# Rope's rotation in a three-layer block: a permutation product on TensorE, or four transfers inside SBUF

## The reference

```python
def apply_rope(x, cos, sin):
    half = HEAD_DIM // 2                     # HEAD_DIM is 64
    x1, x2 = x[..., :half], x[..., half:]
    c, s = cos[None, :, None, :], sin[None, :, None, :]
    out = jnp.concatenate([x1 * c - x2 * s, x2 * c + x1 * s], axis=-1)
    return out.astype(x.dtype)

for i in range(DEPTH_2):                     # 2
    hn = rmsnorm_2(h, norm_g[i])
    if i % N_MIXERS == 0:
        q, k, v, z = split_proj(hn, w_in_a[j], N_KV_A)      # 16 heads of queries, 2 of keys
        q, k = apply_rope(q, cos, sin), apply_rope(k, cos, sin)
        o = sliding_window_sink_attention(q, k, v, sinks_a[j])
    else:
        q, k, v, z = split_proj(hn, w_in_b[j], N_KV_B)      # 16 heads of queries, 4 of keys
        q, k = apply_rope(q, cos, sin), apply_rope(k, cos, sin)
        o = moba_attention(q, k, v)          # causal attention at this length
    h = h + (o * silu(z)) @ w_out[i]
return rmsnorm_2(h, final_g)
```

## Time and profile before

| | |
|---|---|
| Time, 3 runs | 797.45 us median (796.12 to 802.04) |
| Profiled execution | 795.86 us, span 793.9 us |
| TensorE busy | 733.2 us (92% of the span) |
| VectorE busy | 542.9 us (68%) |
| ScalarE busy | 366.6 us (46%) |
| GpSimd busy | 128.7 us (16%) |
| Window layer | about 557 to 672 us of the span |
| Causal layer | about 672 to 782 us |

### The profile page before, as it was taken

One profiled execution on the slowest core, in us unless ns is written; L12 is line 12 of the kernel. 1 busy time (PEld: TensorE's weight loads), 2 busy tenths in 40 slices (PEclk: granted clock), 3 DMA queues, 4 the chain that ended last, 5 costly groups with the idle time before them and its releaser, 6 DMA issues.

```text
span 793.9 us, 14919 instructions
## 1 busy us (share of the span) xinstructions
PE 733.2 (92%) x6112; PEld 685.8 (86%) x6112; DVE 542.9 (68%) x783; ACT 366.6 (46%) x564; POOL 128.7 (16%) x81
## 2 busy tenths in 40 slices
PE   5699999999977999887999999999999988999984
PEld 4489999999976898777999999999888778988884
DVE  3588979777785437667559548456789966788841
ACT  4253334433443436625434343436666665565532
POOL 0053111332222724221005000001300000000000
PEclk9799999999986999988999999999999999999998
DMA  9997799876658767335657664745443334343301
GB/s 308 349 304 239 237 350 301 267 248 213 224 185 288 248 226 248 108 124 172 209 184 265 212 192 133 253 163 158 137 130 107 107 106 159 112 155 109 104 2 53
DMA packets 132455, 152.64 MB, mean 192 GB/s; under 512 B 2616, under 2 KB 126268, under 8 KB 132284
## 3 DMA queue, kind: packets, MB, share of 16 engines
q1 hardware_dynamic: 132324, 152.01, 58.9%
q10 hardware_dynamic: 88, 0.02, 0.0%
HBM read 150.97 MB, written 1.05 MB: 191 GB/s over the span
## 4 chain that ended last, share of the span: by engine, by line
PE 68%; DVE 15%; ACT 10%; issue 4%; DMA 2%; POOL 0%; SPq 0%; DVEq 0%; ACTq 0%; POOLq 0%
PE sc L1353 10%; PE sc L1355 10%; PE sc L1354 10%; PE acc L1353 9%; PE acc L1355 8%; PE acc L1354 8%; DVE wlo L911 5%; ACT whi L601 3%; PE stat L1364 2%; DVE prob L1088 2%; DMA ada<-in_w_ada_dram 2%; ACT probT L734 1%; PE tp L1404 1%; ACT prob L727 1%; DVE prob L1108 1%
## 5 line engine op out<-in xcount | busy, mean ns | idle before, releaser
L911 DVE TENSOR_TENSOR wlo<-raw,whi 128x2048 fp32r<-128x2048 f32 x105 | 258.2, 2463 | 113.1 <-ACT whi L601 112.9
L601 ACT ACTIVATE whi<-raw 128x2048 fp32r<-128x2048 f32 x105 | 200.2, 1908 | 74.6 <-PE sc L1355 61.2
L1353 PE MATMUL sc<-nhi,whi 128*128 128x256 f32 x704 | 200.0, 284 | 6.0 <-DVE nlo L944 4.1
L1354 PE MATMUL sc<-nlo,whi 128*128 128x256 f32 x704 | 198.6, 282 | 0.0
L1355 PE MATMUL sc<-nhi,wlo 128*128 128x256 f32 x704 | 198.6, 282 | 0.0
L1353 PEld LDWEIGHTS sc<-nhi,whi 128*128 128x128 f32 x704 | 134.0, 190 | 7.4 <-issue 4.5
L1354 PEld LDWEIGHTS sc<-nlo,whi 128*128 128x128 f32 x704 | 135.6, 193 | 0.0
L1355 PEld LDWEIGHTS sc<-nhi,wlo 128*128 128x128 f32 x704 | 134.6, 191 | 0.0
L1353 PE MATMUL acc<-nhi,whi 128*128 128x256 f32 x376 | 110.8, 295 | 5.6 <-DVE nlo L944 2.7
L519 POOL TENSOR_TENSOR ada<-ada,cpad 128x2048 f32<-128x2048 f32 x16 | 73.3, 4583 | 244.0 <-DMA ada<-in_w_ada_dram 244.0
L1354 PE MATMUL acc<-nlo,whi 128*128 128x256 f32 x376 | 105.6, 281 | 0.0
(11 more groups left out here) (209 smaller groups left out, 1151.8 us busy)
## 6 DMA issues: line engine op xcount, KB each, us to landing
ada<-in_w_ada_dram SPq DMA_DIRECT2D x28, 1024.0 KB, 5.2
raw<-in_w_gate_dram SPq DMA_DIRECT2D x22, 1024.0 KB, 5.9
raw<-in_w_up_dram SPq DMA_DIRECT2D x22, 1024.0 KB, 5.5
raw<-in_w_down_dram SPq DMA_DIRECT2D x22, 1024.0 KB, 4.9
raw<-in_w_out_dram SPq DMA_DIRECT2D x12, 1024.0 KB, 5.1
raw<-in_w_in_b_dram SPq DMA_DIRECT2D x10, 1024.0 KB, 5.1
raw<-in_w_in_a_dram SPq DMA_DIRECT2D x9, 1024.0 KB, 5.4
raw<-in_w_in_dram SPq DMA_DIRECT2D x8, 1024.0 KB, 7.8
```

Source lines behind the costliest of these rows:

```text
L601: nc.scalar.activation(whi[:, u % NS], raw[:, u % NS], ACT.Copy).then_inc(hi_done, 1)
L911: nc.vector.tensor_tensor(wlo[:, u % NS], raw[:, u % NS], whi[:, u % NS].bitcast(F32), ALU.subtract).then_inc(lo_done, 1)
L1353: mm(to, stat_hi, mov_hi, start=first, stop=False, skip_group_check=True)
L1354: mm(to, stat_hi, mov_lo, start=False, stop=False, skip_group_check=True)
```

## The change

The matrix and its ten products go. In their place SyncE issues four transfers for each rope (`swap`), each of which moves one block of 32 partitions of `kraw` or `qraw` to its partner's partitions in a piece of `ada`, a buffer that is free by then. The minus sign moves into the table of sines. VectorE's three instructions stay; the second waits for `swap_in` and reads SBUF instead of PSUM. The transfers are issued from the same SyncE program as the weight loads, after the load of unit u + 3 of the query unit u (of the layer's first unit for the keys).

```diff
-    for m in range(P):
-        if m % HD < HD // 2:
-            out[m + HD // 2, C_ROT + m] = -1.0
-        else:
-            out[m - HD // 2, C_ROT + m] = 1.0
...
-    out[:, C_SIN:C_SIN + S] = np.sin(ang)
+    sign = np.where(np.arange(P) % HD < HD // 2, -1.0, 1.0)[:, None]
+    out[:, C_SIN:C_SIN + S] = np.sin(ang) * sign
...
             elif kind in ("ROTK", "ROTQ"):
-                st.update(r=r, p=q if kind == "ROTQ" else first_job)
+                st.update(r=r, p=q if kind == "ROTQ" else first_job, after=(qu if kind == "ROTQ" else first_u) + NS)
...
-        rot_ps = sc[0]
+        swapped = {"ROTK": ada[:, 0, 0:2, :], "ROTQ": ada[:, 0, 2:4, :]}
...
+            def swap(st):
+
+                one = st["mixer"] == "window" and st["kind"] == "ROTK"
+                if one:
+                    sp.wait_ge(k_out, 1)
+                else:
+                    sp.wait_ge(job_out, st["p"] + 1)
+                if st["r"]:
+                    sp.wait_ge(rope_done, st["r"])
+                else:
+                    sp.wait_ge(macc_done, MOD_UNITS)
+                src = kraw if st["kind"] == "ROTK" else qraw
+                to = swapped[st["kind"]]
+                n = 1 if one else 2
+                for q in range(4):
+                    sp.dma_start(to[32 * q:32 * q + 32, 0:n], src[32 * (q ^ 1):32 * (q ^ 1) + 32, 0:n, :]).then_inc(swap_in, 16)
...
                             load_unit(st["u"], in_w[name][:, :, at:at + UC])
                         for a in ada_after.get(st["u"], ()):
                             load_ada(a)
+                        for turn in turns.get(st["u"], ()):
+                            swap(turn)
...
                 nc.vector.tensor_tensor(a, src, co, ALU.mult).then_inc(dve_step, 1)
-                dve.wait_ge(rot_done, st["r"] + 1)
+                dve.wait_ge(swap_in, 64 * (st["r"] + 1))
                 steps[0] += 1
-                link(nc.vector.tensor_tensor(b, ps, si, ALU.mult))
+                link(nc.vector.tensor_tensor(b, turned, si, ALU.mult))
...
-            def rotate(st):
...
-                    mm(rot_ps[:, :], rotation, src[:, :, :].rearrange("p b n -> p (b n)"), start=True,
-                       stop=True).then_inc(rot_done, 1)
...
                 transposes(st, 3)
-                if st["next"]["kind"] == "ROTQ":
-                    rotate(st["next"])
                 values(st, 1)
```

More of the change, by code:

```diff
@@ L88, in mixer_plan @@
         steps = []
-        first_job, first_head, first_pair, first_y, first_rot = p, h, g, y, r
+        first_job, first_head, first_y, first_u = p, h, y, u
         if name == "pool":
@@ L119, in mixer_plan @@
                     st["u"] = u
+                    if kind == "Q":
+                        qu = u
                     u += 1
             elif kind in ("ROTK", "ROTQ"):
-                st.update(r=r, p=q if kind == "ROTQ" else first_job)
+                st.update(r=r, p=q if kind == "ROTQ" else first_job, after=(qu if kind == "ROTQ" else first_u) + NS)
                 r += 1
@@ L280, in build @@
         ident = consts[:, C_IDENT:C_IDENT + P]
-        rotation = consts[:, C_ROT:C_ROT + P]
+        swapped = {"ROTK": ada[:, 0, 0:2, :], "ROTQ": ada[:, 0, 2:4, :]}
         cos2 = cos_r.unsqueeze(1).to_broadcast([P, 2, S])
@@ L343, in build @@
         z_done = sem("z_done")
-        rot_done = sem("rot_done")
+        swap_in = sem("swap_in")
         rope_done = sem("rope_done")
@@ L451, in _ @@
                 first = f == 0
+                if not first:
+                    ada_after = {}
                 if first:
@@ L481, in _ @@
                                  3 * FB + 6: (27,), 3 * FB + 7: (28,), 3 * FB + 10: (29,), 3 * FB + 11: (30, 31)}
+                turns = {}
+                for st in [] if first else PLANS["window"] + PLANS["causal"]:
+                    if st["kind"] in ("ROTK", "ROTQ"):
+                        turns.setdefault(st["after"], []).append(st)
                 for name in ("pool",) if first else ("window", "causal"):
@@ L1062, in rope @@
                 if one:
-                    src, ps = kraw[:, 0], rot_ps[:, 0:S]
+                    src, turned = kraw[:, 0], swapped["ROTK"][:, 0]
                     a, b, to, co, si = rope_c[:, 0], rope_s[:, 0], kraw[:, 0], cos_r, sin_r
@@ L1066, in rope @@
                     src = kraw[:, :, :] if st["kind"] == "ROTK" else qraw[:, :, :]
-                    ps = rot_ps[:, :].rearrange("p (b n) -> p b n", b=2)
+                    turned = swapped[st["kind"]]
                     a, b, co, si = rope_c, rope_s, cos2, sin2
@@ L1513, in token_columns @@
                 ins.then_inc(rcol_sum, 1)
-            def rotate(st):
-                if st["mixer"] == "window" and st["kind"] == "ROTK":
-                    pe.wait_ge(k_out, 1)
-                else:
-                    pe.wait_ge(job_out, st["p"] + 1)
-                if st["r"]:
-                    pe.wait_ge(rope_done, st["r"])
-                if st["h_before"]:
-                    pe.wait_ge(sm_read, st["h_before"])
-                if st["kind"] == "ROTK" and st["mixer"] == "window":
-                    mm(rot_ps[:, 0:S], rotation, kraw[:, 0], start=True, stop=True).then_inc(rot_done, 1)
-                else:
-                    src = kraw if st["kind"] == "ROTK" else qraw
-                    mm(rot_ps[:, :], rotation, src[:, :, :].rearrange("p b n -> p (b n)"), start=True,
-                       stop=True).then_inc(rot_done, 1)
             def scores(st, heads):
@@ L1685, in mixer @@
                         job(st)
-                    elif kind in ("ROTK", "ROTQ"):
-                        if before["kind"] != "TPV":
-                            rotate(st)
                     elif kind == "SC":
@@ L1829, in y_chunk @@
     return st["local"] // 2 + n + (4 if st["mixer"] == "pool" else 0)
-def heads_before_rotations():
-    done = 0
-    for name in ("pool", "window", "causal"):
-        for st in PLANS[name]:
-            if st["kind"] == "TPV":
-                done = st["h"] + 4
-            elif st["kind"] in ("ROTK", "ROTQ"):
-                st["h_before"] = done
-heads_before_rotations()
 _INS = ["x", "c", "w_ada", "b_ada", "g_ffn1", "w1_gate", "w1_up", "w1_down", "g_mix", "w_in", "w_pool",
```

## The result

The changed kernel takes 810.9 us in the median of four runs (808.69 to 814.95), the kernel before 797.05 us beside it (796.12 to 802.04): a ratio of 1.018, interval 1.014 to 1.022. It is slower, and by about three times as much as forecast. The profiled execution took 808.69 us, span 806.8.

The account below looks back on a forecast made before the run. The prediction took VectorE and ScalarE to bound the attention steps, with TensorE's products mostly hidden. Its places summed to +4.55 us, which on the median of 797.45 us gave 802.0 us, range 798.0 to 808.5.

Parts of the forecast that it names:

- What bounds the kernel: In the attention layers' steps Q1 and Q2 the chain runs through VectorE and ScalarE, and TensorE's product is hidden.
- L: Time from the end of ScalarE's copy until VectorE can use the turned query: 3.2 us, bounds 2.3 to 4.3.
- The price of a swap: Each rope's swap: 0.07 us for semaphores, 1.23 for three issue spacings of 0.41, 1.9 for landing, 3.2 us together.
- rival B: A swap is dearer: L of 3.8 to 4.3 us, sum 3.6 to 6.6 us larger, 806 to 810 us; chance 16%.
- The landing as a constant: Every swap's landing was taken as 1.9 us, range 1.3 to 2.7; the 7.3 us tail was priced for loads only.
- The queue: Swaps stand before weight loads on SyncE; W4, C4 and C5 are near, and nothing beyond C5 is lost.
- -0.4: Causal's keys and Q0: the swap comes 2.3 us earlier, mostly given back by C5's load queued behind it; -0.4 us.
- Rival C: Swaps cost as forecast but loads behind them come late: 2 to 4 us more, 804 to 806 us; chance 10%.
- Q3 of causal: The product on the chain goes, winning some 0.3 us, and 1.5 us before OUTC cover VectorE's 0.84: -0.3 us.
- TensorE has slack: At Q2 of window TensorE waited for the query's copy at each such product, so it has slack; no cost given.
- +4.55: Forecast sum in us of all places' gains and losses in the two attention layers, window and causal.
- A (in time): Rival: L is 2.4 us or less, VectorE never waits in steps 1 to 3, 797 us; chance 12%.

Follow-up runs that it names:

- e2: Changed kernel with the queries' swaps issued but not waited for, the sine product reading the raw query: ratio 0.999 to the kernel before.
- e3: Changed kernel with only the keys swapped and the queries not turned at all, by product or transfer: ratio 0.997 to the kernel before.
- e10: As e7, but GpSimd instead of ScalarE issues the other two transfers, at all queries but window's Q0: ratio 1.008 to the kernel before.
- e9: Changed kernel with 32 small matmuls more at the start of TensorE's program: ratio 1.026 to the kernel before.
- e6: Changed kernel with each swap one weight load later in SyncE's order: ratio 1.015 to the kernel before.
- e5: Changed kernel with 64 small matmuls more at the start of TensorE's program: ratio 1.021 to the kernel before.
- e7: As e6, with two of each query swap's four transfers issued by ScalarE right behind its copy: ratio 1.013 to the kernel before.
- e13: Changed kernel with 16 matmuls more in each gate step of the attention layers, filling TensorE's pause before the scores: ratio 1.023 to the kernel before.
- e14: e6 with VectorE's previous gate and split between cosine and sine product at Q1 to Q3, plus e13's filling matmuls: ratio 1.014 to the kernel before.

## Why the prediction was wrong

**What bounds the kernel** held: the chain runs through VectorE and ScalarE, rope's result is wanted 2.4 us after the copy, the product was hidden, and L decides most of it. The direction was right. e2 shows that without the wait the kernel is where it was, and e3 that no rotation of the queries at all gains only 2.7 us.

**The price of a swap** is the first step that failed, in the term "two issues in a row start 0.41 us apart". I took it from the start of the load at 262.47 to that of the next issue, where the first of two issues took 0.37 us. The second row of that group says 0.58 for an issue that stands directly behind another, and that is the one to use for the second to fourth of a group: three spacings of 0.6 us are 1.8 and not 1.23. The landing, 1.9 us as my middle value, came out at 2.0 to 2.1. L was 3.9 instead of 3.2, inside the bounds of 2.3 to 4.3, in rival B's range. The six places that move with L make 4.2 us of it. The Trainium skill (DMA: Bandwidth & Descriptors, "Anatomy of one DMA") has 2.0 us as the fixed cost on GpSimd's path; here SyncE's transfers inside SBUF take 2.0 us, and GpSimd's own in e10 2.0 to 2.3 where they aren't late, so the trace agrees with its size, and doesn't show the relief that its remark on HBM would allow, since the write of 256 KB to HBM took 2.2.

**The landing as a constant** is the second. I took the load of 7.3 us as a danger for loads alone. The swaps have such a tail as well, and it hit three of eight: +1.5, +1.4 and +0.7 us, 3.6 in all. In the kernel before ScalarE waits for no load, so such packets cost nothing there. Which swaps are hit depends on where the packets fall (in e9 a single other one, by 1.2 us), so the 3.6 us are partly chance.

**The queue** was followed unit by unit, and only for C5 and C4 was it near. The swap's first issue came as soon as forecast behind the keys' rope (688.83), but C5's load was issued 2.45 us behind it instead of 1.64 and took 5.4 us instead of 5.1; -0.4 became +1.3, of which 0.4 goes with TensorE's slower clock behind the wait. Rival C named the place and had 2 to 4 us for it, where 1.7 were measured. C4's load made ScalarE wait 1.15 us, which the forecast didn't have; that such a wait costs nothing, it had.

**Q3 of causal** was to give back 0.3 us, since the product was on the chain and OUTC had 1.5 us of slack. The place became +1.7. The sine product came 2.3 us later than before, and only 1.0 of these was won back: TensorE paused 1.51 us before the scores and carried the delay on, and OUTC (768.32) followed TensorE's own work, not the gate's product (767.81). Where L was 3.9 (e9), 0.5 us was left at this point. The last 0.4 of the 1.7 lies behind the last landing, in SyncE's closing instructions; its cause is open.

**TensorE has slack** is the step that I didn't price at all. Its pauses became longer, and the granted clock fell behind some of them. Window's output section took 0.85 us more with a fall in it, and 0.15 us more at most in every kernel with the clock at 1.00 there. In causal the fall at 700 to 708 stands behind a pause of 2.67 us that ends with VectorE's row maxima, late by C5's low part: 0.4 us at the next low part and 0.5 at Q1. In e6, where C5 isn't late, the pause, the fall and both delays are gone. The other two falls, at window's Q0 and Q2, cost nothing.

In sum: 4.2 (L), 3.6 (late landings), 1.7 (C5), 1.3 (output section and Q1 of causal, which go with the clock), 1.3 (Q3 of causal without its lateness) and 0.4 spread over the rest are the 12.5 us between +4.55 and +17.0. From 17.0 in the stretch to 14 us by the ratio, 3 us must lie outside it: in the two traces the part ahead was 4.1 us shorter after than before with the same code, and it differs by up to 6 us between traces. Whether the change has a part in that isn't shown.

**The rivals.** A (in time) was excluded by L. B gave 806 to 810 us and comes nearest; C happened beside it. I had priced them one at a time, as if only one could come true, and so the range ended where one did.

**L1095 from SBUF** takes 0.69 us, as forecast.

## What to carry to other kernels

Before an engine's product is replaced by a transfer, compare the transfer's whole latency with the time between the operand's copy and its first use, not with the product's duration: here 3.9 us stood against 2.4, while the products removed were worth 2.7 us in all (e3). Count every issue of a group by the row of one that stands directly behind another, and add a tail to each landing that someone waits for. When unknown costs hit the same waiting engine, add them before setting the range, since they come true together; and where a wait makes TensorE pause, look at the granted clock behind it.

## What the hardware showed that I had not expected

- A swap in whose window an instruction packet was moved came 0.6 to 1.5 us later in 13 of 14 cases of four transfers by SyncE; without one, 26 swaps agree within 0.08 us.
- A 64 KB transfer inside SBUF on 32 partitions takes 2.0 us from issue to landing, nearly the 2.2 us of 256 KB to HBM; SyncE starts four in a row 0.6 us apart, and ScalarE stands still for 1.5 us for two.
- Behind three of its pauses before scores (2.83, 2.21 and 2.67 us) TensorE's granted clock fell, for some microseconds to the lower of its two levels (0.5, that is 1.2 GHz), where the kernel before stays at 1.00. A pause of 2.10 us at 738 us, and one of 1.81 us at Q2 of window in e6, had no fall behind them, and the fall at 652 to 660 had no pause over 1.1 us in the 15 us ahead of it. So which pause costs the clock can't be told from its length alone.
- TensorE's pause at the start of causal is 2.0 to 2.5 us in every kernel here, the one before included. The clock fell at it in five of the sixteen traces (e3, e5, e7, e13, e14), and causal's start took 1.0 to 1.1 us longer in these. So part of what a fall costs comes and goes with any change of the code, and a difference of 1 us between two stretches is to be read only beside the granted clock of both.
